# First three weight chunks of a hybrid LRU/attention layer multiplied together, slice by slice of x, with the LRU gates issued later

## The chip, the cores and the metric

The kernel runs on one core of a Trainium2 chip. The metric is the device time of one execution in microseconds, the median of the runs shown; one more execution was taken by the hardware profiler, and all views of the trace are of that one. Engines are called by their names or as the profile shortens them: TensorE (PE), VectorE (DVE), ScalarE (ACT), GpSimd (POOL), SyncE (SP, which only issues transfers here).

## The reference: one layer, three kinds of heads behind one input projection

With x of 512 tokens by 1024 channels:

```
h    = rmsnorm(x) * norm_g
proj = h @ w_in                       # 1024 -> 4896 columns: u, z, queries, keys, values, gate logits ...
# (A) RG-LRU on 512 channels
xc   = conv_b + sum_k shift(u, k) * conv_w[k]          # causal, width 4
r, i = sigmoid(blockdiag(xc, wa) + ba), sigmoid(blockdiag(xc, wx) + bx)
a    = exp(-8 * r * softplus(-lam));  b = sqrt(1 - a^2) * i * xc
y_A  = scan(h_t = a_t * h_{t-1} + b_t) * silu(z)
# (B) sparse attention of 8 heads (compressed, selected, window), RMS-normed queries and keys
# (C) forgetting attention of 8 heads
out  = x + concat(y_A, y_B, y_C) @ w_out
```

## The kernel before: a hand-written order on five engines

**Projection.** The 4896 columns are cut into 39 chunks of 128 channels, in the order CHUNKS: four u chunks (0 to 3, the LRU input), fg (4, the 8 forget and 24 branch gate logits), kc, vc (5, 6), ks, kw (7, 8), nq 0 to 3 (9 to 12), vn (13, 14), zl (15 to 18), then the attention of group B and later chunks. For fp32 precision each weight chunk is split into a high part wh (a ScalarE copy to fp32r, split(c), L502) and a low part wl = raw - wh (VectorE, split_low(c), L767). x is split the same way into xh (ScalarE, L634) and xl (VectorE, L981). project(c) on TensorE makes 24 matmuls, three for each of the eight slices k of 128 rows of the contraction: wh*xh, wh*xl, wl*xh (L1110 to L1112). They accumulate in one of three PSUM banks, which VectorE must read (evac(c), L745, times rstd) before project(c+3) may write it. raw has 3 slots and wh, wl have 4 (SyncE's load_w(c) waits until split_low(c-3) is done).

**Head of the kernel.** x arrives in eight transfers of 256 KB, weight chunk 0 after the fourth of them, chunks 1 and 2 behind the last. Squares of x come from VectorE (five) and GpSimd (three); TensorE sums each over the channels with a matmul by ones (L1253, into the bank MEAN). ScalarE takes the square root (L639), VectorE the reciprocal (L1004, rstd_bc). project(0) starts behind the eight L1253 matmuls.

**LRU chunks.** For u chunk j, VectorE evacuates to u_pad, ScalarE makes the first tap (L522, xc), VectorE three more taps (L756, conv_done). gates_of(j) on TensorE makes four matmul records (L1129, L1130) behind project(j+1). ScalarE then makes two sigmoids and a tanh (after(j), L544 to L547). Each engine runs its own list in program order. ScalarE's for step c of the loop is:

```
split(c + AHEAD)            # AHEAD = 3
before(c)                   # first tap of chunk c, or the Square of a normed chunk
after(c - 1)                # waits for gates_of(c - 1), then two sigmoids and tanh
if c == AT["kc", 0]: ...    # the batch: sqrt x4, table load, log-sigmoid, Ln and Exp x4
```

VectorE's for step c is before(c) (evac and the taps), after(c-1) (norms), pieces of the LRU tail by the table TAIL_AT (for each u chunk a half 0, L827 and L828, and a half 1, L830 to L832), and last split_low(c + AHEAD).

**Normed chunks.** For ks, kw and nq, ScalarE squares the evacuated chunk (L534), and TensorE sums it over the head (head_mean(c-1), L1121) inside project(c), after 15 of its 24 matmuls.

Of the kernel before, what the change touches and what calls it, by code (L numbers as in the profile page):

```python
# [18 lines left out]
F32 = mybir.dt.float32  # L19
# [3 lines left out]
ALU = mybir.AluOpType  # L23
# [63 lines left out]
POOL_SQUARES = (1, 3, 5)  # L87
VECTOR_SQUARES = tuple(k for k in range(KT) if k not in POOL_SQUARES)

# [3 lines left out]
def program(nc, xT, x_tok, w_in, w_out, chan, const, lru_w, cmp_w, out):  # L93
    ctx = ExitStack()
    with ctx:
# [102 lines left out]
        xh_ready, xl_ready, x_sq = sem("xh_ready"), sem("xl_ready"), sem("x_sq")  # L198
        x_sq_pool, x_sq_used = sem("x_sq_pool"), sem("x_sq_used")
        std_ready = sem("std_ready")  # L200
# [59 lines left out]

        def pool_square(k):
            return (sq, work, std)[POOL_SQUARES.index(k)][:, :]

# [120 lines left out]
        def _(sp):  # L384
            def load_w(c):
# [5 lines left out]
                sp.dma_start(raw[:, c % RAW, :], src).then_inc(raw_loaded[c % RAW], 16)  # L391

            def stack(c):
# [19 lines left out]
            for k in range(KT):  # L413
                sp.dma_start(x_raw[:, k, :], xT[:, k, :]).then_inc(x_loaded[k], 16)
                if k == 0:
                    sp.dma_start(chn[:, :], chan).then_inc(chan_loaded, 16)
                if k == KT // 2 - 1:
                    load_w(0)
            load_w(1)
            load_w(2)  # L420
# [4 lines left out]
            sp.wait_ge(x_sq, len(VECTOR_SQUARES))  # L425
            sp.wait_ge(x_sq_pool, len(POOL_SQUARES))
            sp.dma_start(lru_w_sb[:, :, :, :], lru_w).then_inc(lru_w_loaded, 16)
# [21 lines left out]
        def _(pool):  # L449
# [9 lines left out]
            nc.gpsimd.memset(v_blocks[:, :, :], 0.0).then_inc(small_consts, 1)  # L459
            for k in POOL_SQUARES:  # L460
                pool.wait_ge(x_loaded[k], 16)
                nc.gpsimd.tensor_tensor(pool_square(k), x_raw[:, k, :], x_raw[:, k, :], ALU.mult).then_inc(x_sq_pool, 1)
            def scale_probs(first, last):
# [30 lines left out]
        def _(act):  # L494
            link = chain(lambda: act, "act_chain")

            def split(c):
                if c >= N_STREAM:
                    return
                act.wait_ge(raw_loaded[c % RAW], 16 * (c // RAW + 1))  # L500
                wait_slot(act, c)
                act.activation(wh[:, c % HL, :], raw[:, c % RAW, :], ACT.Copy).then_inc(wh_ready, 1)  # L502
# [129 lines left out]
            for k in range(KT):  # L632
                act.wait_ge(x_loaded[k], 16)
                act.activation(xh[:, k, :], x_raw[:, k, :], ACT.Copy, scale=ch("norm_g", k)).then_inc(xh_ready, 1)  # L634
                if k == KT // 2:
                    split(0)
            split(1)
            act.wait_ge(x_sq_used, KT)
            act.activation(rstd_bc[:, :], MEAN[:, :], ACT.Sqrt, bias=eps1[:, :], scale=1.0 / D).then_inc(std_ready, 1)  # L639
            split(2)  # L640
            for c in range(NSA_END):
# [13 lines left out]
                read_tokens(c, MIDDLE, NT)  # L655
                if c == AT["kc", 0]:

# [51 lines left out]
        def _(dve):  # L709
# [261 lines left out]
            for k in range(KT):  # L971
                dve.wait_ge(x_loaded[k], 16)
                if k in VECTOR_SQUARES:
                    i = VECTOR_SQUARES.index(k)
                    if i >= 2:
                        dve.wait_ge(x_sq_used, VECTOR_SQUARES[i - 2] + 1)
                    dve.tensor_tensor(qr[:, i % 2, :], x_raw[:, k, :], x_raw[:, k, :], ALU.mult).then_inc(x_sq, 1)
                if k == 0:
# [3 lines left out]
                                         ALU.mult, ALU.subtract).then_inc(xl_ready, 1)  # L982
                if k == KT // 2 + 1:
                    split_low(0)
            split_low(1)

# [12 lines left out]
            link(dve.tensor_tensor(csp[:, 0, :], csp[:, 0, :], csp[:, 1, :], ALU.add))  # L999
            dve.tensor_scalar(csp[:, 0, :], csp[:, 0, :], 4.0, None, ALU.mult).then_inc(csp_ready, 1)  # L1000
            dve.wait_ge(x_sq_used, KT)
            dve.memset(u_pad[:, :, 0:CONV - 1], 0.0)
            dve.wait_ge(std_ready, 1)
            dve.reciprocal(rstd_bc[:, :], rstd_bc[:, :]).then_inc(rstd_ready, 1)  # L1004
            dve.wait_ge(rstd_ready, 1)
            split_low(2)
            for c in range(NSA_END):
# [3 lines left out]

                if c == AT["kc", 0]:
                    dve.wait_ge(rstd_T, 1)
                    dve.tensor_copy(rstd_col[:, :], AUX_B[:, :].rearrange("p (t c) -> p t c", t=NT)[:, :, 0])\
                       .then_inc(rcol_ready, 1)
                if c == AT["vc", 0]:
                    branch_gates()
                    log_sigmoid()
                if c == AT["ks", 0]:
# [53 lines left out]
        def _(pe):  # L1073
            def project(c):
# [27 lines left out]
                for k in range(KT):  # L1102
                    if k == KT // 2 + 1 and c - 1 in NORMED:
                        head_mean(c - 1)
                    if k == KT // 2 and c == AT["zl", 0]:
                        cmp_scores(0)
                    if c == 0:
                        pe.wait_ge(xl_ready, k + 1)
                    hi, lo = wh[:, slot, k * P:k * P + m], wl[:, slot, k * P:k * P + m]
# [134 lines left out]
            pe.wait_ge(ones_ready, 1)  # L1244
            for k in range(KT):
                if k in POOL_SQUARES:
                    pe.wait_ge(x_sq_pool, POOL_SQUARES.index(k) + 1)
                    square = pool_square(k)
                else:
                    i = VECTOR_SQUARES.index(k)  # L1250
                    pe.wait_ge(x_sq, i + 1)
                    square = qr[:, i % 2, :]
                pe.matmul(MEAN[:, :], ones[:, :], square, start=(k == 0),  # L1253
                          stop=(k == KT - 1)).then_inc(x_sq_used, 1)
            for c in range(NSA_END):
# [3 lines left out]
                if c == AT["kc", 0]:  # L1259
                    pe.wait_ge(rstd_ready, 1)  # L1260
# [147 lines left out]
```

## Time and profile before

| | |
|---|---|
| median of 3 runs | 484.26 us (483.78 to 484.54) |
| profiled execution | 484.85 us |
| its span in the trace | 483.0 us |
| TensorE busy | 454.1 us |
| VectorE, ScalarE, GpSimd busy | 306.7, 250.1, 74.8 us |
| mean granted TensorE clock | 0.982 |

The span is what the trace covers from the first to the last instruction; the profiled execution took 1.85 us more than its span. Idle time of an engine is wait only where the next engine in the chain needs it.

### The profile page before, as it was taken

To read this page: it belongs to the slowest core of one execution; us is meant where nothing else is said; L and a number is where in the kernel's file an instruction comes from. 1 tells how busy PE (TensorE), PEld (TensorE's weight loads), DVE (VectorE), ACT (ScalarE), POOL (GpSimd) and SP (SyncE) were. 2 spreads that over 40 slices of the span, in tenths; PEclk is the share of its full clock that TensorE was granted. 3 is DMA by queue.
4 is the path that set the end of the run, shared out by engine and by line. 5 is a ranking of instruction groups with operands and counts; after the bars stand their busy time and mean duration, and the time that the engine had idled before them with its cause. 6 is when DMAs were issued, how large, how long until landed. Compare 5 with 4: busy or idle time off the path is not lost.

```text
span 483.0 us, 6629 instructions
## 1 busy us (share of the span) xinstructions
PE 454.1 (94%) x2328; PEld 344.6 (71%) x2328; DVE 306.7 (63%) x560; ACT 250.1 (52%) x472; POOL 74.8 (15%) x121
## 2 busy tenths in 40 slices
PE   5899999999869989999999999999799996999997
PEld 1476688778758766667577897988666675788885
DVE  5976469887987876676427864757866358522204
ACT  4555684667454665666518864852565434312200
POOL 3001240000000155445400000000354300000000
PEclk9899999999979999999999999999899999899999
DMA  7722234431141200000011243552200002932004
GB/s 262 285 88 88 88 88 130 104 115 45 44 131 43 87 2 3 0 2 2 0 45 43 88 108 112 136 171 85 90 2 1 1 6 82 317 117 88 0 1 174
DMA packets 12960, 39.52 MB, mean 82 GB/s; under 512 B 1792, under 2 KB 2048, under 8 KB 12672
## 3 DMA queue, kind: packets, MB, share of 16 engines
q1 hardware_dynamic: 12928, 39.11, 25.0%
q8 instruction: 19, 0.31, 0.3%
q14 instruction: 13, 0.11, 0.1%
HBM read 32.81 MB, written 2.10 MB: 72 GB/s over the span
## 4 chain that ended last, share of the span: by engine, by line
PE 75%; DVE 14%; issue 4%; ACT 3%; POOL 2%; DMA 1%; SPq 0%; POOLq 0%; DVEq 0%; ACTq 0%
PE bank L1110 10%; PE bank L1112 10%; PE bank L1111 10%; PE bank L1224 6%; PE bank L1206 5%; PE bank L1324 4%; PE bank L1326 4%; PE bank L1325 4%; PE bank L1194 3%; PE bank L1198 3%; PE bank L1121 2%; DVE wl L767 2%; PE bank L1090 2%; PE bank L1140 2%; PE bank L1092 2%
## 5 line engine op out<-in xcount | busy, mean ns | idle before, releaser
L1110 PE MATMUL bank<-xh,wh 128*128 128x512 f32 (+1 forms) x264 | 112.4, 426 | 0.0
L1112 PE MATMUL bank<-xh,wl 128*128 128x512 f32 (+1 forms) x264 | 104.2, 395 | 0.0
L1111 PE MATMUL bank<-xl,wh 128*128 128x512 f32 (+1 forms) x264 | 103.8, 393 | 0.0
L767 DVE TENSOR_TENSOR wl<-raw,wh 128x1024 fp32r<-128x1024 f32 x51 | 62.0, 1220 | 33.9 <-ACT wh L502 33.5
L502 ACT ACTIVATE wh<-raw 128x1024 fp32r<-128x1024 f32 x51 | 53.1, 1049 | 34.9 <-PE bank L1326 34.6
L951 DVE TENSOR_REDUCE negmax<-bank 128x1 f32<-128x128 f32 (+3 forms) x96 | 46.1, 484 | 29.4 <-PE bank L1198 26.7
L1110 PEld LDWEIGHTS bank<-xh,wh 128*128 128x128 f32 (+1 forms) x264 | 49.7, 188 | 15.2 <-issue 5.0
L1111 PEld LDWEIGHTS bank<-xl,wh 128*128 128x128 f32 (+1 forms) x264 | 49.6, 188 | 14.6 <-issue 4.2
L1112 PEld LDWEIGHTS bank<-xh,wl 128*128 128x128 f32 (+1 forms) x264 | 49.4, 187 | 11.8
L610 ACT ACTIVATE probs<-bank,negmax 128x256 f32<-128x256 f32 (+3 forms) x77 | 40.5, 527 | 22.0 <-DVE negmax L951 20.6
L470 POOL TENSOR_SCALAR probs<-probs,rcp,gates 128x128 f32<-128x128 f32 (+3 forms) x52 | 31.7, 617 | 127.3 <-DVE rcp L965 126.8
L1324 PE MATMUL bank<-wh,yh 128*128 128x512 f32 x96 | 38.4, 400 | 4.3 <-DVE qr L745 4.3
L1325 PE MATMUL bank<-wl,yh 128*128 128x512 f32 x96 | 38.5, 401 | 0.0
L1326 PE MATMUL bank<-wh,yl 128*128 128x512 f32 x96 | 38.5, 401 | 0.0
L1206 PE MATMUL bank<-cst,probs 128*128 128x128 f32 x192 | 35.0, 280 | 2.9 <-POOL probs L470 2.3
L958 DVE COPY pT<-bank 128x128 f32<-128x128 f32 (+2 forms) x72 | 30.0, 416 | 2.0 <-PE bank L1206 1.5
L1090 PE MATMUL bank<-wh,xh 128*128 128x256 f32 x96 | 28.5, 297 | 1.4 <-ACT v_nsa L592 1.4
L1206 PEld LDWEIGHTS bank<-cst,probs 128*128 128x128 f32 x192 | 22.7, 142 | 8.8 <-POOL probs L470 6.8
L745 DVE TENSOR_TENSOR qr<-bank,rstd_bc 128x512 f32<-128x512 f32 (+1 forms) x23 | 15.8, 688 | 20.0 <-PE bank L1112 19.9
L1092 PE MATMUL bank<-wh,xl 128*128 128x256 f32 x96 | 26.9, 280 | 0.0
L1091 PE MATMUL bank<-wl,xh 128*128 128x256 f32 x96 | 26.9, 280 | 0.0
L1194 PE MATMUL bank<-kh_nsa,q_nsa 128*128 128x128 f32 (+3 forms) x64 | 25.6, 399 | 0.6 <-ACT probs L610 0.6
(200 smaller groups left out, 794.0 us busy)
## 6 DMA issues: line engine op xcount, KB each, us to landing
raw<-in_w_in SPq DMA_DIRECT2D x39, 512.0 KB, 3.3
raw<-in_w_out SPq DMA_DIRECT2D x12, 512.0 KB, 3.8
x_raw<-in_xT SPq DMA_DIRECT2D x8, 256.0 KB, 6.7
x_res<-in_x_tok SPq DMA_DIRECT2D x1, 2048.0 KB, 8.5
out_y<-y_out SPq DMA_DIRECT2D x8, 256.0 KB, 2.1
cmp_w_sb<-in_cmp_w SPq DMA_DIRECT2D x1, 1024.0 KB, 10.7
kh_fox<-kh_fox SPq DMA_DIRECT2D x8, 128.0 KB, 2.4
kl_fox<-kl_fox SPq DMA_DIRECT2D x8, 128.0 KB, 2.5
```

Source lines behind the costliest of these rows:

```text
L502: act.activation(wh[:, c % HL, :], raw[:, c % RAW, :], ACT.Copy).then_inc(wh_ready, 1)
L610: act.activation(probs_of(u, 0, n), SCORE[u % S_RING][:, 0:n], ACT.Exp, bias=negmax[:, u % M_RING:u % M_RING + 1], accum_out=rsum[:, q % R ...
L767: dve.tensor_tensor(wl[:, c % HL, :], raw[:, c % RAW, :], wh[:, c % HL, :].bitcast(F32), ALU.subtract).then_inc(wl_ready, 1)
L951: dve.tensor_reduce(negmax[:, s % M_RING:s % M_RING + 1], SCORE[s % S_RING][:, 0:n], AX.X, ALU.max, negate=True).then_inc(max_ready, 1)
L1110: pe.matmul(dst, hi, xh[:, k, :], start=(k == 0), stop=False)
L1111: pe.matmul(dst, hi, xl[:, k, :], start=False, stop=False)
L1112: mm = pe.matmul(dst, lo, xh[:, k, :], start=False, stop=(k == KT - 1))
L1194: pe.matmul(dst[:, 0:n], q, kh[:, 0:n], start=True, stop=False)
L1206: mm = pe.transpose(PT[u % PTB][:, cols], probs_of(u, j * P, (j + 1) * P), ident)
L1324: pe.matmul(dst, yh[:, e, toks], wh[:, c % HL, cols], start=(e == 0), stop=False)
L1325: pe.matmul(dst, yh[:, e, toks], wl[:, c % HL, cols], start=False, stop=False)
L1326: mm = pe.matmul(dst, yl[:, e, toks], wh[:, c % HL, cols], start=False, stop=(e == ET - 1))
```

## The change: what it does

- **Loads.** Weight chunks 0 to 2 no longer come as whole chunks. Their columns for two slices k at a time (three chunks by 256 columns, 384 KB, pieces of 1 KB) come as a slab behind x slices 0, 2, 4 and 6.
- **Squares.** Even slices are squared by VectorE, odd ones by ScalarE, each into a buffer of its own. GpSimd squares none.
- **First three chunks.** first_chunks() replaces project(0) to project(2) and the loop of L1253: for each slice k it makes nine matmuls (three for each chunk), and sum-of-squares matmuls in between by SQUARES_BEHIND. The last slice is done chunk by chunk.
- **VectorE.** split_low(3) comes ahead of the reciprocal, evac(0) to evac(2) together behind it, then split_low(4); split_low(5) comes ahead of the taps of chunk 1.
- **Gates.** gates_of(0) moves from behind project(1) to the middle of project(4), gates_of(1) from behind project(2) to behind project(4), gates_of(2) from behind project(3) to behind project(5), gates_of(3) from behind project(4) to the middle of project(6).
- **What follows the gates.** ScalarE's batch moves from step kc to step vc, the transposes of rstd from kc to vc, log_sigmoid() behind VectorE's split_low(9), and TAIL_AT moves later.

```diff
-TAIL_AT = (AT["vc", 0], AT["vc", 0], AT["ks", 0], AT["ks", 0], AT["kw", 0], AT["nq", 0], AT["vn", 0], AT["vn", 0])
+TAIL_AT = (AT["ks", 0], AT["ks", 0], AT["kw", 0], AT["kw", 0], AT["nq", 0], AT["nq", 1], AT["vn", 0], AT["vn", 0])
+FIRST = 3
+SLAB = 2
+SQUARES_BEHIND = ((1,), (2, 3), (4, 5), (6,), (7,), (), (), ())
+GATES_AT = ((AT["fg", 0], True), (AT["fg", 0], False), (AT["kc", 0], False), (AT["vc", 0], True))
...
+                src = w_in[0:FIRST, :, i * SLAB * P:(i + 1) * SLAB * P].rearrange("c p q -> p c q")
+                sp.dma_start(slab(raw, i), src).then_inc(slab_loaded[i], 16)
...
             for k in range(KT):
                 act.wait_ge(x_loaded[k], 16)
                 act.activation(xh[:, k, :], x_raw[:, k, :], ACT.Copy, scale=ch("norm_g", k)).then_inc(xh_ready, 1)
-                if k == KT // 2:
-                    split(0)
-            split(1)
+                if k % SLAB == 0:
+                    i = k // SLAB
+                    act.wait_ge(slab_loaded[i], 16)
+                    last = i == KT // SLAB - 1
+                    act.activation(slab(wh, i), slab(raw, i), ACT.Copy).then_inc(wh_ready if last else slab_high,
+                                                                               FIRST if last else 1)
+                else:
+                    act.activation(square_of(k), x_raw[:, k, :], ACT.Square).then_inc(x_sq_act, 1)
             act.wait_ge(x_sq_used, KT)
             act.activation(rstd_bc[:, :], MEAN[:, :], ACT.Sqrt, bias=eps1[:, :], scale=1.0 / D).then_inc(std_ready, 1)
-            split(2)
...
-                split(c + AHEAD)
+                if c + AHEAD >= FIRST:
+                    split(c + AHEAD)
...
-                if c == AT["kc", 0]:
+                if c == AT["vc", 0]:
 
                     act.wait_ge(lru_tau, LRU_T)
...
-                evac(c)
+                if c >= FIRST:
+                    evac(c)
+                if c == 1:
+                    split_low(FIRST + 2)
                 if kind == "u":
...
+            split_low(FIRST)
             dve.wait_ge(x_sq_used, KT)
             dve.memset(u_pad[:, :, 0:CONV - 1], 0.0)
             dve.wait_ge(std_ready, 1)
             dve.reciprocal(rstd_bc[:, :], rstd_bc[:, :]).then_inc(rstd_ready, 1)
             dve.wait_ge(rstd_ready, 1)
-            split_low(2)
+            for c in range(FIRST):
+                evac(c)
+            split_low(FIRST + 1)
...
-                split_low(c + AHEAD)
+                if c + AHEAD > FIRST + 2:
+                    split_low(c + AHEAD)
+                if c == AT["vc", 0]:
+                    log_sigmoid()
...
+                    if k == KT // 2 and (c, True) in GATES_AT:
+                        gates_of(GATES_AT.index((c, True)))
...
+                for k in range(KT):
+                    i = k // SLAB
...
+                    if k < KT - 1:
+                        for c in range(FIRST):
+                            pe.matmul(proj_bank(c)[:, :], wh[:, c, cols], xh[:, k, :], start=(k == 0), stop=False)
...
+                    for x in SQUARES_BEHIND[k]:
+                        mean_square(x)
+
+            first_chunks()
+            for c in range(FIRST, NSA_END):
                 project(c)
-                if c >= 1 and CHUNKS[c - 1][0] == "u":
-                    gates_of(CHUNKS[c - 1][1])
-                if c == AT["kc", 0]:
+                for j, (at, middle) in enumerate(GATES_AT):
+                    if at == c and not middle:
+                        gates_of(j)
+                if c == AT["vc", 0]:
                     pe.wait_ge(rstd_ready, 1)
                     pe.wait_ge(const_loaded, 16)
                     pe.wait_ge(lru_sig, 2 * LRU_T)
```

## Rows read from the trace of the kernel before

**Rows 1.** The page: span, and busy time of each engine.

```profile
span 483.0 us, 6629 instructions
PE 454.1 (94%) x2328; PEld 344.6 (71%) x2328; DVE 306.7 (63%) x560; ACT 250.1 (52%) x472; POOL 74.8 (15%) x121
```

**Rows 2.** Stretches: width, busy time and instructions of each engine, clock, DMA, GB/s.

```profile
18.28:37.75 19.47, 19.47 (x79) 14.87 (x78) 14.63 (x22) 9.38 (x11) 1.73 (x1) 0.97 0.39 128
65.74:77.80 12.06, 12.06 (x51) 9.31 (x52) 11.72 (x20) 8.11 (x13) 0.09 (x1) 1.00 0.16 37
105.15:136.92 31.77, 25.65 (x158) 21.68 (x156) 26.58 (x51) 19.17 (x34) 0.00 (x0) 0.97 0.25 83
```

**Rows 3.** Chain that ended last, in order of time: start, length, what.

```profile
2.10 6.00 DMA x_raw<-in_xT
...
31.38 0.86 PE bank L1130 x2
...
37.75 0.86 PE bank L1129 x2
...
53.03 0.86 PE bank L1130 x2
...
74.88 0.86 PE bank L1121 x2
```

**Rows 4.** TensorE's timeline: sums of squares in the head, transpose at zl 0.

```profile
4.60 2.05 PE L1253 MATMUL bank<-qr,ones 128*128 128x512 f32 x2 [4.60 <-DVE qr L977]
...
15.65 3.62 PE L1253 MATMUL bank<-qr,ones 128*128 128x512 f32 x4 [1.89 <-DVE qr L977]
...
136.92 0.69 PE L1165 MATMUL bank<-cst,qr 128*128 128x128 f32 x2 [4.76 <-DVE qr L897]
```

**Rows 5.** A stretch of the loads, same columns as Rows 2.

```profile
5.00:8.00 3.00, 3.00 (x4) 0.60 (x3) 1.95 (x2) 0.94 (x2) 1.04 (x1) 1.00 0.92 246
```

**Rows 6.** VectorE's timeline: start, length, line, operands.

```profile
20.32 3.33 DVE L1004 RECIPROCAL rstd_bc<-rstd_bc 128x512 f32<-128x512 f32 x1
...
26.54 2.33 DVE L756 SCALAR_TENSOR_TENSOR xc<-u_pad,chn,xc 128x512 f32<-128x512 f32 x3 [0.89 <-ACT xc L522]
...
39.36 3.33 DVE L756 SCALAR_TENSOR_TENSOR xc<-u_pad,chn,xc 128x512 f32<-128x512 f32 x3 [0.88 <-ACT xc L522]
...
67.37 0.69 DVE L827 SCALAR_TENSOR_TENSOR u_pad<-tau,xc 128x512 f32<-128x512 f32 x1
...
71.42 1.20 DVE L767 TENSOR_TENSOR wl<-raw,wh 128x1024 fp32r<-128x1024 f32 x1
...
105.12 0.69 DVE L745 TENSOR_TENSOR qr<-bank,rstd_bc 128x512 f32<-128x512 f32 x1 [0.72 <-PE bank L1112]
```

**Rows 7.** ScalarE's timeline behind the first gates.

```profile
32.32 1.28 ACT L544 ACT_TABLE_LOAD   x1 [0.22 <-PE bank L1130]
33.62 0.69 ACT L544 ACTIVATE tau<-bank,chn 128x512 f32<-128x512 f32 x1
...
35.55 1.04 ACT L502 ACTIVATE wh<-raw 128x1024 fp32r<-128x1024 f32 x1
```

**Rows 8.** ScalarE's timeline behind the last gates, through the batch.

```profile
53.93 0.69 ACT L544 ACTIVATE tau<-bank,chn 128x512 f32<-128x512 f32 x1 [4.22 <-PE bank L1130]
...
55.85 1.05 ACT L502 ACTIVATE wh<-raw 128x1024 fp32r<-128x1024 f32 x1
...
58.14 1.28 ACT L661 ACT_TABLE_LOAD   x1
...
69.36 1.99 ACT L502 ACTIVATE wh<-raw 128x1024 fp32r<-128x1024 f32 x2
73.26 0.63 ACT L534 ACTIVATE sq<-qr 128x512 f32<-128x512 f32 x1 [1.91 <-DVE qr L745]
```

**Rows 9.** Two stretches at the lower clock, columns of Rows 2.

```profile
135.30:142.10 6.80, 5.18 (x21) 4.89 (x22) 6.30 (x15) 5.02 (x7) 0.00 (x0) 0.50 0.43 136
...
343.50:347.00 3.50, 3.32 (x13) 2.65 (x13) 3.16 (x8) 1.58 (x5) 2.44 (x4) 0.51 0.23 89
```

More of the change, by code:

```diff
@@ L198, in program @@
         xh_ready, xl_ready, x_sq = sem("xh_ready"), sem("xl_ready"), sem("x_sq")
-        x_sq_pool, x_sq_used = sem("x_sq_pool"), sem("x_sq_used")
+        x_sq_act, x_sq_used = sem("x_sq_act"), sem("x_sq_used")
+        slab_loaded = [sem(f"slab_loaded{i}") for i in range(KT // SLAB)]
+        slab_high, slab_low = sem("slab_high"), sem("slab_low")
         std_ready = sem("std_ready")
@@ L259, in stack_copies, with square_of, slab @@
             return sum(0 if CHUNKS[x][0] in ("nq", "fq") else 4 for x in NORMED[:c])
-        def pool_square(k):
-            return (sq, work, std)[POOL_SQUARES.index(k)][:, :]
+        def square_of(k):
+            return y_lru[:, k // 2, :] if k % 2 else (qr[:, 0, :], qr[:, 1, :], sq[:, :], std[:, :])[k // 2]
+        def slab(x, i):
+            return x[:, 0:FIRST, i * SLAB * P:(i + 1) * SLAB * P]
         def half_of(s):
@@ L424, in _ @@
             sp.wait_ge(xl_ready, KT)
-            sp.wait_ge(x_sq, len(VECTOR_SQUARES))
-            sp.wait_ge(x_sq_pool, len(POOL_SQUARES))
+            sp.wait_ge(x_sq, KT // 2)
+            sp.wait_ge(x_sq_act, KT // 2)
             sp.dma_start(lru_w_sb[:, :, :, :], lru_w).then_inc(lru_w_loaded, 16)
@@ L499, in split @@
                     return
-                act.wait_ge(raw_loaded[c % RAW], 16 * (c // RAW + 1))
+                act.wait_ge(raw_loaded[c % RAW], 16 * (c // RAW))
                 wait_slot(act, c)
@@ L972, in _ @@
                 dve.wait_ge(x_loaded[k], 16)
[L973 to L977, printed above, removed]
+                if k % 2 == 0:
+                    dve.tensor_tensor(square_of(k), x_raw[:, k, :], x_raw[:, k, :], ALU.mult).then_inc(x_sq, 1)
                 if k == 0:
@@ L982, in _ @@
                                          ALU.mult, ALU.subtract).then_inc(xl_ready, 1)
-                if k == KT // 2 + 1:
-                    split_low(0)
-            split_low(1)
+                if k % SLAB == 0:
+                    i = k // SLAB
+                    last = i == KT // SLAB - 1
+                    if last:
+                        dve.wait_ge(wh_ready, FIRST)
+                    else:
+                        dve.wait_ge(slab_high, i + 1)
+                    dve.tensor_tensor(slab(wl, i), slab(raw, i), slab(wh, i).bitcast(F32),
+                                      ALU.subtract).then_inc(wl_ready if last else slab_low, FIRST if last else 1)
             dve.wait_ge(const_loaded, 16)
@@ L1017, in _ @@
                     branch_gates()
-                    log_sigmoid()
                 if c == AT["ks", 0]:
@@ L1244, in _, with mean_square @@
             pe.wait_ge(ones_ready, 1)
[L1245 to L1248, printed above, removed]
-                else:
[L1250 to L1253, printed above, removed]
+            def mean_square(k):
+                if k % 2 == 0:
+                    pe.wait_ge(x_sq, k // 2 + 1)
+                else:
+                    pe.wait_ge(x_sq_act, k // 2 + 1)
+                pe.matmul(MEAN[:, :], ones[:, :], square_of(k), start=(k == 0),
@@ L1254, in _, with first_chunks @@
                           stop=(k == KT - 1)).then_inc(x_sq_used, 1)
-            for c in range(NSA_END):
+            def first_chunks():
+                mean_square(0)
+                for k in range(KT):
+                    i = k // SLAB
+                    last = i == KT // SLAB - 1
+                    pe.wait_ge(xh_ready, k + 1)
+                    if last:
+                        pe.wait_ge(wh_ready, FIRST)
+                    else:
+                        pe.wait_ge(slab_high, i + 1)
+                    cols = slice(k * P, (k + 1) * P)
+                    if k < KT - 1:
+                        for c in range(FIRST):
+                            pe.matmul(proj_bank(c)[:, :], wh[:, c, cols], xh[:, k, :], start=(k == 0), stop=False)
+                    pe.wait_ge(xl_ready, k + 1)
+                    if k < KT - 1:
+                        for c in range(FIRST):
+                            pe.matmul(proj_bank(c)[:, :], wh[:, c, cols], xl[:, k, :], start=False, stop=False)
+                    if last:
+                        pe.wait_ge(wl_ready, FIRST)
+                    else:
+                        pe.wait_ge(slab_low, i + 1)
+                    for c in range(FIRST):
+                        if k == KT - 1:
+                            pe.matmul(proj_bank(c)[:, :], wh[:, c, cols], xh[:, k, :], start=False, stop=False)
+                            pe.matmul(proj_bank(c)[:, :], wh[:, c, cols], xl[:, k, :], start=False, stop=False)
+                        mm = pe.matmul(proj_bank(c)[:, :], wl[:, c, cols], xh[:, k, :], start=False, stop=(k == KT - 1))
+                        if k == KT - 1:
+                            mm.then_inc(proj_done, 1)
+                    for x in SQUARES_BEHIND[k]:
+                        mean_square(x)
```

16 lines of the change are left out of this document (4 added, 12 removed).

## The prediction, made before the changed kernel ran

> **What bounds the kernel now.** I read the page first: TensorE is busy 454.1 of 483.0 us and no other engine comes near [rows 1], so what TensorE does not wait for is free, and what it waits for is paid. Next the chain in order of time: from the first projection matmuls to 105 us it is TensorE without a break, through all u chunks, their gates, kc, vc, ks, kw, nq 0 and nq 1 [rows 3]; the stretch from 65.74 to 77.80 is busy for all its 12.06 us [rows 2]. Then the stretches: from 105.15 to 136.92 TensorE is busy for only 25.65 of 31.77 us [rows 2], where VectorE's norms and low parts lead up to the first transpose of the compressed branch, which TensorE reaches at 136.92 after an idle 4.76 us [rows 4]. Last the timelines of VectorE and ScalarE, for the order of work behind the gates [rows 6 to 8]. Two things follow. Time saved in the head passes on to the end if nothing new makes TensorE wait. And a new wait of TensorE ahead of 105 us is paid in full.
>
> **Unit prices.** The stretch 65.74 to 77.80 is two chunks, 48 matmuls, and one fp32 sum over the head of 0.86 us, so a projection matmul comes each (12.06 - 0.86) / 48 = 0.233 us, a chunk 5.6 us, half a chunk 2.8 us [rows 2, 3]. An fp32 matmul of 512 columns is 0.86 us (two records) and one gates_of is two of them, 1.72 us [rows 3]. At the lower clock the fp32 one is 1.81 us: four records, two matmuls, in 3.62 us [rows 4].
>
> **Term 1, the head: -4.0 us.** Before, the three chunks and gates 0 end at 37.75 [rows 3], so without the gates at 36.0. After, TensorE does the first sum of squares from 4.60 to about 6.4 at the lower clock [rows 4], then waits for slab 0. Slab 0 lies behind 295 KB and brings the sum to 679 KB. A transfer that brings it to 807 KB before, x slice 2, landed at 8.10 [rows 3], and nothing can start before 6.4; I take 7.1 for the landing, as the loads run at 246 GB/s there [rows 5], plus 0.8 us for ScalarE's split of 768 columns (1.04 us for 1024 [rows 7]), so TensorE goes on at 7.9. From there it needs 72 x 0.233 = 16.8 and seven sums, 6.0 us, 22.8 in all, and some of it at the lower clock: before, the four records from 15.65 ran at it after a wait of 1.89 us [rows 4]. I charge 1.3 us. End: 32.0. Bounds: 6.4 + 22.8 + 1.0 = 30.3, and, with the slab as late as x slice 2 was, 8.9 + 22.8 + 2.2 = 33.9. x and the slabs, 3.7 MB, are all in by about 17 us at the rates of the loads; the last square is wanted only at about 25, so 8 us of TensorE's work cover a late or slow slab. The trace of before has no 1 KB pieces: nothing below cost (the same bytes move), and above, 2 us more on the end. I take nothing. The Trainium skill (DMA: Bandwidth & Descriptors, Specifications) puts the smallest piece at line rate at 512 B, so by it the 1 KB pieces cost nothing either; no row here shows it. The squares that leave GpSimd and go to ScalarE cost nothing, since ScalarE has eight copies, four squares and four slab splits, some 13 us of work up to 19 us.
>
> **Term 2, the bank of chunk 3: +0.65 us.** project(3) writes the bank of chunk 0, which VectorE can read only behind the reciprocal. The last sum of squares lies behind slice 4, so 27 matmuls, 6.3 us, follow it. In that time: square root 0.6, ScalarE's split(3) 1.05, split_low(3) 1.2, reciprocal 3.33, evac 0.69, together 6.9 [rows 6, 7]. TensorE waits 0.6 to 0.7 us. Bounds 0.3 and 0.9. Here split_low(3) ahead of the reciprocal is what makes it late.
>
> **Term 3, ScalarE's queue behind gates 0: +5.1 us.** Look at program order. ScalarE's step 1 is split(4), first tap 1, after(0); only step 2 has split(5). after(0) waits for gates 0. Before, gates 0 end at 31.38 + 0.86 = 32.24, table load, sigmoids and tanh follow, and split(5) runs from 35.55 to 36.59, that is 4.35 us after the gates [rows 3, 7]. There the low part of chunk 5 was wanted 17 us later. After, VectorE does split_low(5) ahead of the taps of chunk 1, so those taps wait for split(5), and TensorE's gates 1 wait for those taps. From the end of gates 0: split(5) done at 4.35, split_low(5) 1.2 (5.55), taps 2.33 (7.9) [rows 6, 7]. TensorE has only the second half of the fg chunk to do, 2.8 us. It then waits 7.9 - 2.8 = 5.1 us. What is queued behind gates 1 is everything: project(5) and all that follows. With the cover gone nothing hides it. No gain is possible; below the term is 4.5 if the table load runs ahead of the wait, above 6.1, since the taps of chunk 2, at 39.36, took 3.33 us and not 2.33 [rows 6].
>
> From there on: gates 2 and 3 find their taps done (taps 2 are done 2.3 us after taps 1; taps 3 by 15.7 us after gates 0, and gates 3 come 19.7 us after gates 0).
>
> **Term 4, the batch on ScalarE: +5.35 us.** Count from the end of gates 3. Before (53.89) [rows 3]: tau starts at once, split(8), the fg sigmoid, and the batch from 58.14 to 69.36, 4.25 and 15.5 us after; then two splits, and the Square of ks [rows 8]. The sum over the head, which needs that Square, is at 74.88, 21 us after gates 3 [rows 3]. After, gates 3 sit in the middle of vc, and split(9) comes ahead of the batch: the batch starts at 5.25, ends at 16.5, split(10) brings 17.5, the Square 18.1. TensorE has: half of vc 2.8, eight short transposes with a wait of 0.4 for the fg sigmoid, together 4.05, project(7) 5.6, 15 matmuls of project(8) 3.5, so it asks at 13.15. It waits 4.95 us, with the 0.4 5.35. VectorE's evac(7) is done in time (log_sigmoid waits for the batch until about 11.4, evac at 13.2), so ScalarE's queue is what ends last. SyncE's loads of chunks 8 to 10 go by low parts that are done earlier. Bounds 4.5 and 5.8.
>
> **Term 5, the clock: +3.4 us.** After the 4.76 us wait that ends at 136.92 [rows 4], the clock is at its lower level until 142.10, and 5.2 us of work went at half speed: 2.6 us lost. The other such stretch, 343.5 to 347.0, had 3.3 us of work, 1.7 lost [rows 9]. The two new waits are as long as the first of these. I charge each 1.7, between 0.4 and 2.6. The Trainium skill (TensorE: Matmul & The Clock Gate, HAM oscillation) says the same of waits for data, that the array comes back from them at half rate, but its worked example loses only about 0.8 us at each wait; by that the sum would be 1.7 us less, 493.8. The trace here shows more at each of its own waits, so the rows decide.
>
> **Term 6, VectorE at nq: +0.7 us.** A full LRU tail takes VectorE 67.37 to 71.42, 4.05 us, of which the second half is 2.6 [rows 6]. By the new TAIL_AT step nq 0 has a first half in place of a second (-1.15) and nq 1 a second half that it didn't have (+2.6). VectorE is behind TensorE through both steps and has 0.72 us to spare at 105.12 [rows 6]; 1.45 - 0.72 = 0.7 us late into the stretch that VectorE sets. Bounds 0 and 1.45.
>
> **Sum.** -4.0 + 0.65 + 5.1 + 5.35 + 3.4 + 0.7 = +11.2 us. The profiled execution was 484.85 (span 483.0 and 1.85 around it), so 496.1 by it; the median of the runs is 0.6 lower, 495.5. I say 495. The forecast's own range from the bounds, not all at one end: 490 to 499.5.
>
> **Rivals.**
> *Only the first wait.* ScalarE's batch is hidden after all, because the steps between gates 3 and the Square are looser than I count. Then -4.0 + 0.65 + 5.1 + 1.7 + 0.7 = +4.2, 488.4 us. For it: before, the Square could have been done 2.9 us ahead of its use. Against: the sum over the head comes 7.8 us nearer to gates 3.
> *The head's gain is kept.* One mechanism: the split of chunk 5 doesn't hang on gates 0, so neither VectorE nor TensorE queues behind ScalarE's sigmoids, all gates come earlier by the same time, and the batch starts early enough. Then -4.0 + 0.65 + 0.7 = -2.7, 481.6 us. It decides from the point where the two waits together stay under 2.7 us. For it: TensorE had no break before until 105 us. Against: ScalarE's program order, which rows 7 show word for word (tanh, then the split).
> *Slow slabs.* Pieces of 1 KB and a cold clock throughout the head put the end of three chunks at 36 or later: +15 and more, 499.5 to 503. Against: the cover of 8 us.
>
> **How the numbers follow.** Forecast 0.70, only the first wait 0.12, gain kept 0.08, slow slabs 0.06, something within 0.2% of before 0.04 (0.2% is about what a measurement of this kernel can tell from no change). The range takes in the forecast and the first rival: 488 to 499.5. Faster 0.08, same 0.04, slower 0.88.
>
> **What would show it.** In the profile after: the third chunk ends near 32 us; VectorE's reciprocal ends about when slice 7 does; TensorE idle some 5 us ahead of L1129 of gates 1, released by VectorE's taps, and ScalarE idle for 7 us ahead of the first sigmoid; TensorE idle some 5 us ahead of the first sum over the head, released by ScalarE's Square; the clock low behind both. I am wrong if ScalarE has split chunk 5 ahead of its first sigmoid, or if the first sum over the head doesn't wait.

## The result, and the profile after

| | before | after |
|---|---|---|
| median | 484.4 us (483.78 to 485.38, 4 runs) | 499.33 us (497.53 to 500.09, 4 runs) |
| ratio | | 1.0298, 95% interval 1.0273 to 1.0323 |
| span of the profiled execution | 483.0 us | 495.7 us |
| mean granted clock | 0.982 | 0.972 |

The change makes the kernel slower by 3%. The forecast was 495, its range 488 to 499.5: the median lies 0.2 us inside the upper end, and two of the four runs lie above it. The profiled execution after is the fastest of the four (497.53), so its span explains 12.7 us of the 14.9 us between the medians; what the other 2 us are is taken up below.

The page answers [rows 1]. TensorE does the same work in a longer span. It is idle for 39.0 us and was for 28.9, and busy for 2.6 us more:

```profile
span 495.7 us, 6641 instructions
PE 456.7 (92%) x2328; PEld 346.8 (70%) x2328; DVE 301.7 (61%) x560; ACT 251.9 (51%) x477; POOL 70.1 (14%) x118
```

TensorE's three longest waits in the kernel after (engine, line, whom it waited for, us in total, times, longest):

```profile
PE bank L1153 <- DVE xc L772: 5.2, 1, 5.2
PE bank L1189 <- DVE qr L913: 4.9, 1, 4.9
PE bank L1145 <- ACT sq L542: 4.9, 1, 4.9
```

The middle one is the 4.76 us of [rows 4], which both kernels have. The other two are new, each a single wait: gates 1 for VectorE's taps, and the first sum over the head for ScalarE's Square. Where they lie is in TensorE's timeline, which answers [rows 3, 4]:

```profile
4.82 2.04 PE L1274 MATMUL bank<-qr,ones 128*128 128x512 f32 x2 [4.82 <-DVE qr L990]
6.43 1.72 PE L1291 MATMUL bank<-xh,wh 128*128 128x512 f32 x3
...
31.07 0.50 PE L1134 MATMUL bank<-xh,wh 128*128 128x512 f32 x1 [0.80 <-DVE u_pad L758]
...
49.20 2.07 PE L1153 MATMUL bank<-xc,lru_w_sb 128*128 128x512 f32 x2 [5.15 <-DVE xc L772]
...
68.72 0.46 PE L1326 MATMUL bank<-cst,std 64*128 64x64 f32 x4 [0.49 <-ACT std L561]
...
83.20 1.72 PE L1145 MATMUL bank<-sq,cst 128*128 128x512 f32 x2 [4.86 <-ACT sq L542]
...
147.77 0.69 PE L1189 MATMUL bank<-cst,qr 128*128 128x128 f32 x2 [4.92 <-DVE qr L913]
```

Read with [rows 3, 4], the milestones are these. project(3) starts at 31.07; before, the three chunks without gates 0 ended at 36.0: 5.0 us won. The first sum over the head is at 83.20 and was at 74.88: 8.3 us behind. From there to the first transpose of the compressed branch 64.6 us pass, and before it was 62.0: 2.5 more. From there to the end of the span, 347.9 and 346.1: 1.8 more. Together 12.7. The loss is made in the stretch between 31 and 83 us, which takes 13.3 us more than before.

ScalarE's timeline behind gates 0, and behind the last gates, answers [rows 7, 8]:

```profile
41.38 1.28 ACT L552 ACT_TABLE_LOAD   x1 [7.87 <-PE bank L1154]
...
44.60 1.04 ACT L510 ACTIVATE wh<-raw 128x1024 fp32r<-128x1024 f32 x1
...
70.39 1.28 ACT L674 ACT_TABLE_LOAD   x1
...
81.59 1.04 ACT L510 ACTIVATE wh<-raw 128x1024 fp32r<-128x1024 f32 x1
82.53 0.61 ACT L542 ACTIVATE sq<-qr 128x512 f32<-128x512 f32 x1
```

And VectorE's, which answers [rows 6]:

```profile
25.78 1.23 DVE L783 TENSOR_TENSOR wl<-raw,wh 128x1024 fp32r<-128x1024 f32 x1 [6.81 <-ACT wh L510]
26.95 3.34 DVE L1024 RECIPROCAL rstd_bc<-rstd_bc 128x512 f32<-128x512 f32 x1
...
45.68 1.23 DVE L783 TENSOR_TENSOR wl<-raw,wh 128x1024 fp32r<-128x1024 f32 x1 [9.37 <-ACT wh L510]
46.82 3.77 DVE L772 SCALAR_TENSOR_TENSOR xc<-u_pad,chn,xc 128x512 f32<-128x512 f32 x5
```

(The last row merges the taps of chunk 1 with the first two of chunk 2.) ScalarE sits idle for 7.87 us, while TensorE works on project(3) and half of project(4). VectorE sits idle for 9.37 us, through half of project(4), gates 0 and the first 1.6 us of TensorE's own wait. No engine is short of time: three engines queue behind each other. ScalarE waits for gates 0, VectorE for the split that stands behind the sigmoids in ScalarE's list, and TensorE for the taps that stand behind the low part in VectorE's.

The stretches at the lower clock (columns of [rows 2], they answer [rows 9]):

```profile
45.97:52.80 6.83, 3.60 (x5) 1.54 (x6) 5.87 (x8) 0.38 (x1) 0.00 (x0) 0.51 0.22 78
83.50:86.93 3.43, 3.43 (x8) 2.09 (x7) 1.77 (x2) 1.91 (x4) 0.00 (x0) 0.51 0.70 207
145.00:155.20 10.20, 7.43 (x27) 6.66 (x28) 8.99 (x24) 7.21 (x8) 0.00 (x0) 0.50 0.34 118
```

The granted clock is half of the full one in each, so half of TensorE's busy time in each is lost: 1.8, 1.7 and 3.7 us. The third was 2.6 before [rows 9].

### The profile page after: what moved, and what is told of

Same layout as the page of the kernel before. It is cut to its first block, busy times and chain, and to the rows that moved or that the text cites. A ratio compares the mean times of both kernels' runs of the same rounds, so it can differ in the third digit from the quotient of the medians.

```text
span 495.7 us, 6641 instructions
## 1 busy us (share of the span) xinstructions
PE 456.7 (92%) x2328; PEld 346.8 (70%) x2328; DVE 301.7 (61%) x560; ACT 251.9 (51%) x477; POOL 70.1 (14%) x118
## 4 chain that ended last, share of the span: by engine, by line
PE 67%; DVE 17%; ACT 7%; issue 5%; POOL 2%; DMA 1%; POOLq 0%; DVEq 0%; ACTq 0%
PE bank L1134 7%; PE bank L1136 7%; PE bank L1135 7%; PE bank L1248 6%; PE bank L1230 5%; PE bank L1381 4%; PE bank L1382 4%; PE bank L1383 4%; PE bank L1218 3%; PE bank L1222 3%; DVE wl L783 2%; PE bank L1145 2%; PE bank L1274 2%; PE bank L1114 2%; PE bank L1116 2%
## 5 line engine op out<-in xcount | busy, mean ns | idle before, releaser
L1134 PE MATMUL bank<-xh,wh 128*128 128x512 f32 (+1 forms) x240 | 103.3, 431 | 0.9 <-DVE u_pad L758 0.8
L1136 PE MATMUL bank<-xh,wl 128*128 128x512 f32 (+1 forms) x240 | 95.4, 398 | 0.0
L1135 PE MATMUL bank<-xl,wh 128*128 128x512 f32 (+1 forms) x240 | 95.1, 396 | 0.0
L783 DVE TENSOR_TENSOR wl<-raw,wh 128x1024 fp32r<-128x1024 f32 x48 | 58.4, 1221 | 57.6 <-ACT wh L510 57.3
L510 ACT ACTIVATE wh<-raw 128x1024 fp32r<-128x1024 f32 x48 | 50.2, 1049 | 35.8 <-PE bank L1383 35.7
L1134 PEld LDWEIGHTS bank<-xh,wh 128*128 128x128 f32 (+1 forms) x240 | 45.8, 191 | 16.1 <-issue 5.5
L1135 PEld LDWEIGHTS bank<-xl,wh 128*128 128x128 f32 (+1 forms) x240 | 45.5, 190 | 13.5 <-issue 4.0
L1136 PEld LDWEIGHTS bank<-xh,wl 128*128 128x128 f32 (+1 forms) x240 | 45.4, 189 | 10.9
```

The costliest lines, as they stand in the source:

```text
L783: dve.tensor_tensor(wl[:, c % HL, :], raw[:, c % RAW, :], wh[:, c % HL, :].bitcast(F32), ALU.subtract).then_inc(wl_ready, 1)
L1134: pe.matmul(dst, hi, xh[:, k, :], start=(k == 0), stop=False)
L1135: pe.matmul(dst, hi, xl[:, k, :], start=False, stop=False)
L1136: mm = pe.matmul(dst, lo, xh[:, k, :], start=False, stop=(k == KT - 1))
```

## The experiments

All are compared with the kernel before on the same chip, by the ratio of the medians. The kernel after is at 1.0298.

### ScalarE splits chunk 5 ahead of its first sigmoids

```diff
-                if c + AHEAD >= FIRST:
-                    split(c + AHEAD)
+                if c != 2:
+                    split(c + AHEAD)
+                if c == 1:
+                    split(2 + AHEAD)
                 before(c)
```

> The changed kernel with one edit: ScalarE makes the high part of chunk 5 in step 1, ahead of the sigmoids of gates 0, and no longer in step 2. If ScalarE's queue behind gates 0 is the cause of the first wait (my theory), the 5.15 us that TensorE idled ahead of gates 1 at 49.20 go to under 0.5 us, the lower clock from 45.97 to 52.80 goes too, and the time falls by 5 to 8 us, to 491.5 to 494.5; the second wait, ahead of the first sum over the head, stays at 4.9 us. Rival: the taps of chunk 1 are late because VectorE has too much in front of them (evacs and low parts together); then the wait keeps 3 us or more and the time stays above 497.

Measured: 492.94 us, ratio 1.0165 (1.0137 to 1.0193), 1.3% or 6.4 us less than after. ScalarE's timeline of this kernel:

```profile
33.23 1.99 ACT L510 ACTIVATE wh<-raw 128x1024 fp32r<-128x1024 f32 x2
...
42.84 1.28 ACT L552 ACT_TABLE_LOAD   x1 [6.91 <-PE bank L1156]
```

Both splits run some 8 us ahead of the sigmoids, TensorE has no wait ahead of gates 1 and no low clock there. The wait for the Square is the same 4.86 us. Moving one line in ScalarE's list takes the first wait away.

### The Ln and Exp of the batch behind the Square of ks

```diff
                 before(c)
+                if c == AT["ks", 0]:
+                    for j in range(LRU_T):
+                        act.wait_ge(lru_ix, j + 1)
+                        link(act.activation(xc[:, j, :], tau[:, j, :], ACT.Ln, bias=one1[:, :]))
+                        act.activation(xc[:, j, :], xc[:, j, :], ACT.Exp, scale=-1.0).then_inc(lru_seed, 1)
...
-                    for j in range(LRU_T):          # in step vc
-                        ...                         # the same three lines
```

> The changed kernel with one edit: of ScalarE's batch, the four pairs of Ln and Exp (5.1 us) run in step ks, behind the Square of ks, and no longer in step vc ahead of it. If the batch in ScalarE's queue is the cause of the second wait (my theory), the 4.86 us ahead of the first sum over the head at 83.20 go to about 1 us (the evac of ks, at 78.1 to 78.8, then ends last), the lower clock behind it goes, and the time falls by 4 to 6 us, to 493.5 to 495.5. The first wait stays at 5.1 us. Rival: the LRU tail is the true chain, and VectorE, which now gets the Ln and Exp results later, hands the wait on to low parts and norms: then the time stays within 2 us of 499.

Measured: 495.41 us, ratio 1.0231 (1.0201 to 1.0261), 3.3 us less than after by the ratios. TensorE's timeline:

```profile
49.05 2.07 PE L1154 MATMUL bank<-xc,lru_w_sb 128*128 128x512 f32 x2 [5.14 <-DVE xc L773]
...
79.22 1.13 PE L1146 MATMUL bank<-sq,cst 128*128 128x512 f32 x2 [1.15 <-ACT sq L542]
...
97.64 1.12 PE L1146 MATMUL bank<-sq,cst 128*128 128x512 f32 x2 [1.46 <-ACT sq L542]
...
120.12 0.38 PE L1115 MATMUL bank<-wh,xh 128*128 128x256 f32 x1 [1.49 <-DVE wl L784]
```

The wait goes to 1.15 us as expected and the time lies at the upper end of what was expected, but the gain by the ratios, 3.3 us, is less than the 4 to 6 expected. The rival is right in part: VectorE gets the results later, and waits of 1.46 us (new) and 1.49 us (0.42 after) stand further on.

### Both edits

> Both edits of the two kernels before in one. If the two waits add up independently, the time falls by 9 to 13 us against the changed kernel, to 486.5 to 490.5, which is still above the kernel before. Rival: removing the first wait brings TensorE sooner to the second one, whose length hangs on ScalarE alone, so that the second grows by what the first gave back: then it ends no lower than the better of the two, 493 or more.

Measured: 488.99 us, ratio 1.0096 (1.0076 to 1.0115). The two gains, 1.33% and 0.67%, add up to the 2.02% measured, and the wait for the Square is 1.15 us here too, with the first wait gone: within the intervals the two waits are independent.

### Extra matmuls in the two waits

```diff
                 n = nth_normed(c)
+                if n == 0:
+                    filler(18)
                 pe.wait_ge(sq_ready, n + 1)
...
+            def filler(n):
+                for i in range(n):
+                    pe.matmul(bank[7][:, :], xh[:, i % KT, 0:P], xh[:, i % KT, :], start=True, stop=True)
+
             def gates_of(j):
+                if j == 1:
+                    filler(18)
                 pe.wait_ge(conv_done, j + 1)
```

> The changed kernel with 18 extra matmuls of the projection's form, into a bank that is not in use, ahead of each of the two waits (18 x 0.233 = 4.2 us, less than either wait of 5.15 and 4.86 us). The output is unchanged. The waits stay as they are, only TensorE is not idle in them. If the lower clock behind the waits costs 1.7 us each as in my sum, the granted clock stays at 1.00 from 46 to 53 and from 83.5 to 87 and the time falls by 3 to 4 us, to 495.5. Rival: the slow clock falls mostly into the waits themselves and costs under 1 us in all: then the time stays at 498.5 or more.

Measured: 493.85 us, ratio 1.0187 (1.0165 to 1.0209): 1.1% or 5.4 us less than after, for 36 matmuls more. The same two stretches of this kernel:

```profile
45.97:52.80 6.83, 5.77 (x23) 3.79 (x22) 5.48 (x8) 1.96 (x4) 0.92 (x1) 1.00 0.23 78
83.50:86.93 3.43, 3.43 (x19) 2.54 (x18) 2.26 (x4) 2.77 (x5) 0.00 (x0) 1.00 0.73 231
```

The clock stays full in both. TensorE still gets the taps and the Square when it did, so all that is won is the speed behind the waits. It is more than the 3 to 4 us expected and more than the 3.5 us that the two stretches show in the profile after, which is the fastest run. The mean granted clock of every run is on record: 0.972 in that run and 0.969 in the three others, and 0.983 to 0.986 in the four runs with the extra matmuls. As the lower level is half of the full clock, 0.969 is 31 us of a 497 us span at that level, and 0.983 to 0.986 are 14 to 17 us. With TensorE busy for three quarters of such time, as in the profile after (20.6 of 27.3 us), half of it lost, the difference is worth 5.3 to 6.4 us, an estimate that holds the 5.4 measured.

### VectorE: taps of chunk 1 first, then the low part of chunk 5

```diff
-                if c == 1:
-                    split_low(FIRST + 2)
                 if kind == "u":
                     ...
+                if c == 1:
+                    split_low(FIRST + 2)
```

> The changed kernel with one edit on VectorE: the low part of chunk 5 comes behind the taps of chunk 1, not ahead of them. ScalarE's order stays. My theory of the first wait: two things together, ScalarE's split behind its sigmoids and VectorE's low part ahead of the taps. Then gates 1 find their taps done, but project(5) still wants the low part 4.35 + 1.2 = 5.55 us after gates 0, where TensorE has 2.8 + 1.7 = 4.5 us of work: a wait of about 1.1 us in place of 5.15, no lower clock at 46, and 5 to 7 us less, 492 to 494.5. Rival: ScalarE's late split alone is the cause, wherever VectorE puts the low part: then the wait stays over 4 us and the time above 497.

Measured: 491.61 us, ratio 1.0149 (1.0113 to 1.0185). The expected wait is there, in TensorE's timeline:

```profile
47.54 0.47 PE L1134 MATMUL bank<-xh,wh 128*128 128x512 f32 x1 [1.01 <-DVE wl L783]
```

1.01 us in place of 5.15, and the clock stays full; one more wait of 0.79 us for a low part stands at 55.80. The gain, 1.5% or 7.2 us, is just above the 5 to 7 expected. So the long wait needed both: a late split on ScalarE, and the order on VectorE that put the taps behind it. Either edit undoes it.

### Gates earlier, with the early split

```diff
-GATES_AT = ((AT["fg", 0], True), (AT["fg", 0], False), (AT["kc", 0], False), (AT["vc", 0], True))
+GATES_AT = ((AT["u", 3], False), (AT["fg", 0], True), (AT["fg", 0], False), (AT["kc", 0], True))
```

> The changed kernel with its head and slabs, ScalarE's split of chunk 5 ahead of its first sigmoids, and the gates earlier: gates 0 behind project(3), 1 in the middle and 2 at the end of project(4), 3 in the middle of project(5). The batch stays in step vc. With gates 3 earlier by 8 us, the Square of ks is ready at the time it is asked for (18.1 against 18.4 us after gates 3). If the head is worth what the profile says (the three chunks end at 30.2 and not at 36.0, -5.8, and +0.8 for the bank), no new long wait is left and the kernel beats the one before: 479 to 481.5. Rival: the head's gain is lost by VectorE between ks and zl 0 in any order: 483.5 to 486.

Measured: 483.06 us, ratio 0.9965 (0.9943 to 0.9986). No new long wait is left and it is faster than before, but by 0.35%, not by the 0.6 to 1.1% expected: a miss, between the forecast and the rival. In its trace the head is ahead of before by 3.9 us at project(3), which starts at 32.10, and by 1.4 us at the end: more than half is lost again on the way (see the version with the order of before, below).

### Gates earlier, the split left behind the sigmoids

> The same gates as in the kernel before this one, but ScalarE's split of chunk 5 is left in step 2, behind its first sigmoids. It tells the place of the gates from the order of the queue. If the queue is the cause of the first wait, it stays at about 5 us wherever gates 0 are, ahead of gates 1, with the lower clock behind it, while the wait for the Square is gone: 6 to 8 us above the kernel with the early split, 486 to 489. Rival: that gates 0 sit one chunk late is the cause; then this kernel is within 1.5 us of the one with the early split.

Measured: 489.13 us, ratio 1.0086 (1.0054 to 1.0119), 5.9 us above the early split by the ratios.

```profile
47.25 2.08 PE L1153 MATMUL bank<-xc,lru_w_sb 128*128 128x512 f32 x2 [5.15 <-DVE xc L772]
```

The wait is 5.15 us again with gates 0 a half chunk earlier, to the hundredth the wait of the kernel after. It hangs on the queue, not on the place of the gates. The wait for the Square, which is gone here, does hang on that place.

### Half an LRU tail moved from nq 1 to vn

```diff
-TAIL_AT = (AT["ks", 0], AT["ks", 0], AT["kw", 0], AT["kw", 0], AT["nq", 0], AT["nq", 1], AT["vn", 0], AT["vn", 0])
+TAIL_AT = (AT["ks", 0], AT["ks", 0], AT["kw", 0], AT["kw", 0], AT["nq", 0], AT["vn", 0], AT["vn", 0], AT["vn", 0])
```

> The changed kernel with one edit on VectorE: the second half of the LRU tail of u chunk 2 (2.6 us) moves from step nq 1 to step vn. If VectorE sets the whole stretch from nq 0 to the first transpose of the compressed branch (my theory), the same work is only done later in the same queue, the transpose comes within 0.5 us of where it was and the time is the same within 1 us, 498.5 to 500. Rival: only the norms of nq 1 to nq 3 are what TensorE waits for: then it gets 0.7 to 2.6 us faster.

Measured: 499.71 us, ratio 1.0299 (1.026 to 1.0338), not to be told from the kernel after. VectorE's timeline in step nq 1, TensorE's first transpose, and the stretch of low clock behind the wait for the Square:

```profile
117.32 0.69 DVE L758 TENSOR_TENSOR qr<-bank,rstd_bc 128x512 f32<-128x512 f32 x1 [1.83 <-PE bank L1136]
```

```profile
151.70 0.69 PE L1189 MATMUL bank<-cst,qr 128*128 128x128 f32 x2 [7.50 <-DVE qr L913]
```

```profile
82.50:89.30 6.80, 4.80 (x9) 3.15 (x10) 3.96 (x5) 4.57 (x8) 0.00 (x0) 0.50 0.81 228
```

The median came as expected, the mechanism did not. From the first sum over the head (84.50 here, 83.20 after) TensorE comes to its wait for the transpose after 59.7 us in both, and the wait is 7.50 in place of 4.92 us: it is VectorE that comes 2.6 us later, 0.7 of them through the longer low clock in the last row. The first row says why the rest. Without the half tail VectorE waits 1.83 us for TensorE in step nq 1, where the kernel after has no such wait. So VectorE does not set the whole stretch from nq 0, as I had it. In nq 1 most of the 2.6 us were covered by that idle time, and in vn nothing covers them. The intervals of the two ratios reach 1 to 2 us to either side, so they can't show what this costs in the median.

The last row shows something else. The wait for the Square is 4.86 us here too, yet the low clock behind it lasts 6.8 us and takes 2.4 us, where in the profile after it was 3.4 and 1.7. The same wait costs differently from run to run. That fits a median 1.8 us above the profiled run, since the three other runs of the kernel after have the lower mean clock (0.969 for 0.972, some 3 us more at the lower level); in which stretch they lost it no trace shows.

### The head with the order of before

The version with early gates, and ScalarE's batch back in step kc, log_sigmoid in its old place and the table TAIL_AT of before.

> The kernel with early gates and early split of chunk 5, and now also ScalarE's batch back in step kc, log_sigmoid back where it was, and the LRU tail by the table of before. What is left of the change is its head, and VectorE gets a whole LRU tail (4.05 us) back into step vc, where it idled. If the LRU tail in nq 0 and nq 1 is what the version with early gates still loses, the first transpose of the compressed branch comes 1 us or more sooner against the first sum over the head than there, and the time falls from 483.1 by 1 to 2 us, to 481 to 482. Rival: the evac of ks waits for that tail, and TensorE waits for the Square of ks instead: then 483 or more.

Measured: 482.31 us, ratio 0.9961 (0.9948 to 0.9975), 10 runs. By the ratios it is not to be told from the version with early gates (0.9965); the fall of 1 to 2 us that I expected against it isn't there. TensorE's timeline:

```profile
31.88 0.50 PE L1135 MATMUL bank<-xh,wh 128*128 128x512 f32 x1 [0.80 <-DVE u_pad L760]
...
72.14 1.13 PE L1146 MATMUL bank<-sq,cst 128*128 128x512 f32 x2 [0.87 <-ACT sq L542]
...
134.46 0.69 PE L1190 MATMUL bank<-cst,qr 128*128 128x128 f32 x2 [4.92 <-DVE qr L915]
```

Against before it is ahead by 4.1 us at project(3) (36.0 without gates), by 2.7 at the first sum over the head and by 2.5 at the transpose [rows 3, 4]. So the stretch from there to the transpose is back at 62.3 us, and the rival is right too: the evac of ks comes behind the LRU tail and TensorE waits 0.87 us for the Square.

### The same with extra matmuls at zl 0, and the control

```diff
             def cmp_transpose(t):
+                if t == 0:
+                    for i in range(18):
+                        pe.matmul(bank[7][:, :], xh[:, i % KT, 0:P], xh[:, i % KT, :], start=True, stop=True)
                 pe.wait_ge(cmp_p, t + 1)
```

> The kernel before this one with 18 extra matmuls (4.2 us) ahead of the 4.8 us wait for the first transpose of the compressed branch, which both original kernels have too. Output unchanged. The lower clock behind that wait (135.3 to 142.1 in the kernel before, with 5.2 us of work in it) should go: 2 to 3 us less than without, near 479. Rival: that stretch is set by VectorE, not by TensorE's speed, and the time is the same within 1 us.

> The kernel before the change with the same 18 extra matmuls at the same wait and nothing else: a control of what the filler is worth without the change. If the lower clock costs TensorE 2.6 us there, 482 to 482.5 (0.995 of before). Rival as in the run before: within 0.2% of before.

Measured: 480.09 us, ratio 0.9919 (0.9901 to 0.9937) with the head, and 481.5 us, ratio 0.9949 (0.9932 to 0.9966) in the kernel before with nothing else. The low clock behind that wait is gone in both. It is worth 0.42% and 0.51%, about 2 to 2.5 us. The version with both, the head and the extra matmuls, is the fastest of the study, though 1 us above the 479 expected.

### The reciprocal ahead of split_low(3)

```diff
-            split_low(FIRST)
             dve.wait_ge(x_sq_used, KT)
...
             dve.reciprocal(rstd_bc[:, :], rstd_bc[:, :]).then_inc(rstd_ready, 1)
+            split_low(FIRST)
```

> The kernel with the order of before behind the head (first of this call), with one edit on VectorE: the reciprocal runs ahead of split_low(3), not behind it. My term 2 says that split_low(3) makes the evac of chunk 0 late: the 0.79 us that TensorE waits for it ahead of project(3) should go to 0.1 or less in the trace, and the time fall by at most 0.8 us, less than the runs spread. Rival: project(3) then waits for its low part instead, and the wait stays.

Measured: 481.84 us, ratio 0.9954 (0.9938 to 0.9971), not to be told from 0.9961. VectorE's timeline:

```profile
25.38 3.35 DVE L1025 RECIPROCAL rstd_bc<-rstd_bc 128x512 f32<-128x512 f32 x1 [0.62 <-ACT rstd_bc L652]
28.65 1.16 DVE L785 TENSOR_TENSOR wl<-raw,wh 128x1024 fp32r<-128x1024 f32 x1
29.73 1.88 DVE L760 TENSOR_TENSOR u_pad<-bank,rstd_bc 128x512 f32<-128x512 f32 x3
```

and TensorE starts project(3) at 30.65 with no wait. The 0.8 us were the order of two VectorE instructions, as term 2 said. In its trace TensorE is 1.35 us earlier at the first transpose (133.11 against 134.46), but only 0.3 us at the end of the span (480.3 against 480.6), since its stretches at the lower clock took 7.4 us in place of 6.0; in the median the gain drowns.

## Why the prediction was right, term by term

| term | predicted | profile or runs |
|---|---|---|
| 1 head | -4.0 | -5.8 (the chunks end near 30.27) |
| 2 bank of chunk 3 | +0.65 | +0.80 |
| 3 queue behind gates 0 | +5.1 | +5.15 |
| 4 batch | +5.35 | 0.49 + 4.86 = +5.35 |
| 5 clock | +3.4 | 1.8 + 1.7 = +3.5 in the profile; +5.4 by the filler |
| 6 VectorE at nq | +0.7 | 2.5 less 1.7 of clock, +0.8 |
| in no term | 0 | +1.1 clock at 145 us, +1.0 up to the first sum over the head, +0.7 behind 147.77 |
| sum | +11.2 | +12.7 in the span, +14.9 in the median |

**Terms 3 and 4** carried the sign, and were right to a tenth of a microsecond. Both came from reading three engines' lists in program order and adding row durations from one event on: the end of gates 0, and the end of gates 3. The runs show the causes apart: the split ahead of the sigmoids takes away the first wait alone, the Ln and Exp behind the Square most of the second alone, and both together the sum. That the median still lies in the range is a matter of 0.2 us, less than the runs spread (2.6 us), and in the sum term 1 errs one way and what stands in no term the other: the number owes something to luck, the two waits don't.

**Term 1 was mis-sized**, 1.8 us too small a gain. I put slab 0 at 7.1 and TensorE's restart at 7.9, from the landing of x slice 2, the latest of its neighbours. The row at 6.43 shows TensorE on the slab right behind its first sum of squares, and ScalarE's copy of slab 0 shows that it had landed by 5.46, since no wait for it stands there:

```profile
5.46 0.83 ACT L647 ACTIVATE wh<-raw 128x768 fp32r<-128x768 f32 x1
```

That is 1.5 of the 1.8 us. Of the 1.3 us charged for a lower clock 1.1 are there: the nine matmuls from 6.43 to 9.60 took 3.2 us in place of 2.1. But the granted clock reads 1.00 in that stretch, as it does in [rows 5], so the rows don't show that it is the clock's doing, here or in the first sum of squares. The 1 KB pieces cost nothing that the profile shows: four slabs landed in 6.5 us in the median, the x slices of the same stretch in 6.3. The end at 30.27 is at the very edge of the term's lower bound: 6.4 + 22.8 + 1.0 is 30.2, and not the 30.3 that I wrote down.

**Term 5 was right in the profile and mis-sized over several runs.** The two new waits cost 1.8 and 1.7 us in the profile, as charged, and by the filler 5.4 us, with the clocks of all runs to bear it out. The bounds of the term (up to 2.6 for each wait) held that; the value taken did not. The stretch at 145 us took 3.7 us, 1.1 more than before. That this comes of the change is not shown: behind the same wait, 4.8 to 4.9 us long in the versions without extra matmuls there, the traces have 2.4 to 4.0 us. And two stretches at the lower clock that the trace of before has, in its head (1.7 us lost, [rows 4]) and at 343.5 (1.6 us, [rows 9]), aren't there after, so that over the whole span the clock took 2.6 us more than before. The Trainium skill's 0.8 us for each wait (TensorE: Matmul & The Clock Gate, HAM oscillation) was further off: behind the waits of 4.8 to 5.2 us that lie past the head, the traces show 1.7 to 4.0 us lost where nothing filled them.

**The rivals.** That only the first wait counts is refuted: the second stood at 4.86 us. That the head's gain is kept is refuted for the change and holds for the version with early split and early gates, by 1.7 us of the 2.7 that I gave it. Slow slabs are refuted by the start at 6.43.

**What the sum leaves.** Between project(3) and the first sum over the head the kernel after takes 52.1 us. The same work before took 74.88 - 37.75 and one more pair of gates, 38.85; waits of 10.5 and clock of 1.8 make 51.1. Of the one microsecond left, TensorE's timeline gives 0.4 us to the start of project(6) at 60.33: it waits there for its low part, which VectorE ends at 60.19, behind the taps of chunk 3. The rest is in steps of 0.1 to 0.2 us around the waits and the transposes of rstd. Of the 0.7 us behind 147.77, TensorE's waits for GpSimd's probs grew by 0.7 us (2.3 to 3.0); a low stretch at 421.5 lost 3.0 us where the one at 411.8 lost 1.7 before, and the one at 343.5 is gone (1.6), which nearly cancels. In the trace of the version with the order of before the head is ahead by 4.1 us at project(3), and by 2.4 at the end (1.9 by the ratio of the medians). 0.87 us of what is lost is a wait for the Square of ks; for the rest no experiment was made. Nor was any made that takes the earlier start of the first chunks apart from the loads by slabs, so what each gave of the 5.8 us is open.

## What to carry to other kernels

When work is moved later on one engine, read every other engine's list from the instruction that waits for it: what stands behind it there, in program order, is late too, even when it has nothing to do with it. Here a copy that needed no gates stood behind the sigmoids that did, and one line's place was worth 1.3% of the kernel.

A wait of 5 us on TensorE is priced with what the clock takes afterwards, here 1.7 to 4.0 us, a third to four fifths of the wait again. Matmuls with no use, put into a wait that can't be removed, won 0.4 to 0.5% at one wait in two kernels, and 1.1% at two waits in a third.

A gain in a head is worth what the order behind it lets through: of 5.8 us won in the loads and first chunks, 1.9 us were left in the medians once the gates, the split and the LRU tail were put right.

## What the runs showed of the hardware

The same wait of TensorE, 4.86 us for the Square, was followed by 3.4 us at the lower clock in the profile after, and by 6.8 us in two others (the tail moved to vn, the early split). Behind a much shorter wait, 1.69 us ahead of the scores in the attention, the trace of before has 3.5 us at the lower clock [rows 9], and the kernel after has the same wait and full clock. And 18 matmuls in a wait of 5 us kept the clock full each time, although TensorE was idle for 0.8 to 1.1 us behind them.
